# The delta rule's triangular inverse on packed 32x32 diagonal blocks instead of whole 128x128 tiles

## The chip, the core and the metric

The kernel runs on one core of a Trainium2 chip. The metric is the device time of one execution in microseconds, as the median of several runs. The engines are TensorE (PE; its weight loads are PEld), VectorE (DVE), ScalarE (ACT), GpSimd (POOL) and SyncE (SP, which issues most transfers). Each runs its own list of instructions in order, and they meet at semaphores.

## The reference

It computes one inference step of a two-layer decoder for a prompt of 512 tokens with 16 meta tokens and for 8 samples of 8 tokens. The first layer has sparse attention beside a gated DeltaNet, the second an HGRN2 recurrence; each is followed by a squared-ReLU MLP. The part that matters here is the delta rule, for every chunk and head:

```python
gam = jnp.cumsum(gg, axis=-1)
dec = jnp.exp(jnp.where(incl, gam[..., :, None] - gam[..., None, :], -jnp.inf))
kkt = jnp.einsum('bhtd,bhsd->bhts', kk, kk)
m = jnp.where(strict, bb[..., :, None] * kkt * dec, 0.0) + eye
sol = lax.linalg.triangular_solve(m, rhs, left_side=True, lower=True, unit_diagonal=True)
u, w = sol[..., :dv], sol[..., dv:]
v_new = u - jnp.einsum('bhtd,bhde->bhte', w, S)
```

## The kernel before

All 592 tokens (64 of the samples, 16 meta, 512 of the prompt) lie on the free axis of feature-major tiles. The stages follow one another: projections of layer one, convolution, attention, delta rule, output projection, MLP, the second layer, and again an MLP. The dense products stream 200 weight units of 512 KB from HBM and split each f32 operand into two fp32r halves.

The delta rule treats five token tiles, t = 0 with 80 rows (the samples and the meta tokens) and t = 1 to 4 with 128 rows, and four heads in each. It has three parts.

*Preparation* (`pe_gdn_prep`, `dve_gdn_prep`, `act_gdn_prep`): per tile the decays, the attention products (L694), the key products (L695) and transposed keys (L696). DVE makes the strictly triangular X (L716), ACT the scaled keys kd (L742) after `ebc` (L739). Each engine goes through the tiles in order.

*Inverse* (`pool_inv`, `pe_inv`, `act_inv`, `dve_inv`): the inverse of the triangular matrix I + X is built by doubling. At level l, blocks of 2^l on the diagonal are already inverted, and pairs of them are joined. T is kept as `Ti` and its transpose as `Tt`. A turn is one tile at one level: POOL masks X to the blocks that join (XL, L761), PE forms the first product (L778), ACT evicts it to P1 (L811), PE multiplies by T twice, for both orientations (L797, L799), and DVE subtracts the results from Ti and Tt (L826, L828). Level 0 has one transpose on PE instead (L785) and two subtractions from the identity (L821, L822). Four products of 128x128x128, one a head, make up each step. The list INV holds the turns, level by level and within a level tile by tile; tile 0 ends after level 3, the others after level 6. PE's order is written out: first product of turn n, then second products of turn n - 1. XL and P1 have two buffers, and PSUM banks 0 to 5 serve in pairs.

*Scan* (`pe_gdn_scan` and its partners): it starts at L852 when the whole inverse is done, and carries the state from tile to tile through Tt.

The POOL queue issues the load of the state (`sdelta`) ahead of the masks. The table of constants is loaded once at the start, on ACT's queue.

Of the kernel before, what the change touches and what calls it, by code (L numbers as in the profile page):

```python
# [21 lines left out]
ALU = mybir.AluOpType  # L22
# [3 lines left out]
P = 128  # L26
# [41 lines left out]
LEVELS = 7  # L68
HLEVELS = 7
# [3 lines left out]
def constant_table():  # L73
# [66 lines left out]
def hybrid_step(nc, x, consts, keep, at, w, wsmall, vecs, stconv, sdelta, shgrn, kvpages, ptab,  # L140
                y, krows, vrows, ikrows, convo_p, convo_s, delta_p, delta_s, hgrn_p, hgrn_s):
    ctx = ExitStack()
    with ctx:
# [582 lines left out]

        def act_gdn_prep():
            for t in range(NT):
                R, e = ROWS[t], t % 2
                nc.scalar.wait_ge(sg("gd_col"), t + 1)  # L730
                alink(nc.scalar.activation(G(G_ED)[0:R, t, :], gcol[0:R, t, 4:8], ACT.Exp))
                nc.scalar.activation(egl[:, t, :, 0:nseg(t)],
                                     ps[:, 4, 16:16 + 4 * NSEG].rearrange("p (h s) -> p h s", h=4)[:, :, 0:nseg(t)],
                                     ACT.Exp).then_inc(sg("gd_egl"), 1)
                nc.scalar.wait_ge(sg("gd_dec"), t + 1)
                nc.scalar.activation(dec[e][0:R, :, 0:R], dec[e][0:R, :, 0:R], ACT.Exp).then_inc(sg("gd_ex"), 1)
                if t:
                    nc.scalar.wait_ge(sg("gd_qk"), t)
                nc.scalar.activation(ebc[:, :, 0:R], bank(5, P, R), ACT.Exp).then_inc(sg("gd_ebc"), 1)  # L739
                nc.scalar.wait_ge(sg("gd_c"), t + 1)  # L740
                for hd in range(DNH):
                    ins = nc.scalar.activation(kd[t][0:R, hd, :], bank(0, R)[:, hd], ACT.Copy,  # L742
                                               scale=G(G_ED)[0:R, t, hd:hd + 1])
                ins.then_inc(sg("gd_kd"), 1)

        INV = [(l, t) for l in range(LEVELS) for t in range(NT) if t or l < 4]
        LAST = {t: (3 if t == 0 else LEVELS - 1) for t in range(NT)}

        def pool_inv():
            for n, (l, t) in enumerate(INV):
                R = ROWS[t]
                if l == 0:
                    nc.gpsimd.wait_ge(sg("gd_x"), t + 1)
                if n >= 2 and INV[n - 2][0] == 0:
                    nc.gpsimd.wait_ge(sg("inv_used"), n - 1)
                elif n >= 2:
                    nc.gpsimd.wait_ge(sg("inv_1"), n - 1 - NT)
                m = C(f"lev{l}")[0:R, 0:R].rearrange("p (o c) -> p o c", o=1).to_broadcast([R, 4, R])  # L760
                nc.gpsimd.tensor_tensor(XL[n % 2][0:R, :, 0:R], X[t][0:R, :, 0:R], m, ALU.mult)\  # L761
                    .then_inc(sg("inv_xl"), 1)

        def pe_inv():

            nc.tensor.wait_ge(sg("l2_rt"), 8)
            nc.tensor.wait_ge(sg("gd_kd"), NT)
            for n in range(len(INV) + 1):
                if n < len(INV):
                    l, t = INV[n]  # L770
                    R = ROWS[t]
                    nc.tensor.wait_ge(sg("inv_xl"), n + 1)
                    if l:
                        nc.tensor.wait_ge(sg("inv_used"), INV.index((l - 1, t)) + 1)
                        if n >= 2 + NT:
                            nc.tensor.wait_ge(sg("inv_p1"), n - 1 - NT)
                        for hd in range(DNH):
                            mm = nc.tensor.matmul(bank(n % 2, R, R)[:, hd], XL[n % 2][0:R, hd, 0:R],  # L778
                                                  Ti[t][0:R, hd, 0:R], start=True, stop=True)
                        mm.then_inc(sg("inv_1"), 1)  # L780
                    else:
                        if n >= 2:
                            nc.tensor.wait_ge(sg("inv_used"), n - 1)
                        for hd in range(DNH):
                            mm = nc.tensor.transpose(bank(2 + 2 * (n % 2), R, R)[:, hd], XL[n % 2][0:R, hd, 0:R],  # L785
                                                     C("ident")[0:R, 0:R])
                        mm.then_inc(sg("inv_2"), 1)
# [4 lines left out]
                R = ROWS[t]  # L792
                nc.tensor.wait_ge(sg("inv_p1"), m + 1 - NT)
                nc.tensor.wait_ge(sg("inv_used"), m - 1)
                for hd in range(DNH):
                    if l < LAST[t]:
                        nc.tensor.matmul(bank(2 + 2 * (m % 2), R, R)[:, hd], Tt[t][0:R, hd, 0:R],  # L797
                                         P1[m % 2][0:R, hd, 0:R], start=True, stop=True)
                    mm = nc.tensor.matmul(bank(3 + 2 * (m % 2), R, R)[:, hd], P1[m % 2][0:R, hd, 0:R],  # L799
                                          Tt[t][0:R, hd, 0:R], start=True, stop=True)  # L800
                mm.then_inc(sg("inv_2"), 1)

        def act_inv():
            nc.scalar.wait_ge(sg("gd_qk"), NT)
            for n, (l, t) in enumerate(INV):
                R = ROWS[t]
                if l:
                    nc.scalar.wait_ge(sg("inv_1"), n + 1 - NT)
                    if n >= 2 + NT:
                        nc.scalar.wait_ge(sg("inv_2"), n - 1)  # L810
                    nc.scalar.activation(P1[n % 2][0:R, :, 0:R], bank(n % 2, R, R), ACT.Copy)\  # L811
                        .then_inc(sg("inv_p1"), 1)

        def dve_inv(link):
            for n, (l, t) in enumerate(INV):
                R = ROWS[t]
                nc.vector.wait_ge(sg("inv_2"), n + 1)
                if l == 0:
                    i4 = C("ident")[0:R, 0:R].rearrange("p (o c) -> p o c", o=1).to_broadcast([R, 4, R])
                    nc.vector.wait_ge(sg("inv_xl"), n + 1)  # L820
                    nc.vector.tensor_tensor(Ti[t][0:R, :, 0:R], i4, bank(2 + 2 * (n % 2), R, R), ALU.subtract)  # L821
                    link(nc.vector.tensor_tensor(Tt[t][0:R, :, 0:R], i4, XL[n % 2][0:R, :, 0:R], ALU.subtract),  # L822
                         "inv_used")
                    continue
                if l < LAST[t]:
                    nc.vector.tensor_tensor(Ti[t][0:R, :, 0:R], Ti[t][0:R, :, 0:R], bank(2 + 2 * (n % 2), R, R),  # L826
                                            ALU.subtract)
                link(nc.vector.tensor_tensor(Tt[t][0:R, :, 0:R], Tt[t][0:R, :, 0:R],  # L828
                                             bank(3 + 2 * (n % 2), R, R), ALU.subtract),
                     "inv_used")  # L830

# [11 lines left out]
        def pe_gdn_scan():  # L843
            nc.tensor.wait_ge(sg("inv_used"), len(INV))
# [1335 lines left out]
```

## Time and profile before

| | us |
|---|---|
| median of 3 runs | 2011.22 |
| runs | 2010.89 to 2012.54 |
| profiled execution, its own time | 2011.88 |
| span on the core in it | 2010.1 |
| PE busy | 1811.2 (90%) |
| DVE, ACT, POOL busy | 993.0, 590.2, 281.7 |
| mean granted clock of PE | 0.925 of 2.4 GHz |

Times inside the program are counted from the span's start. A record is one instruction on the trace; an f32 product shows as two PE records with a weight load each, a transpose as one. The duration of a PE record includes its way through the pipeline, so the pace of a run of records is read from their starts.

### The profile page before, as it was taken

The numbers are of one execution on the slowest core, as the hardware profiler recorded it, in microseconds if no ns is written. First come the engines' busy times: TensorE is split into PE (matmuls) and PEld (weight loads), VectorE is DVE, ScalarE is ACT, GpSimd is POOL, SyncE is SP. The second block draws the span as 40 slices with busy tenths as digits, with TensorE's granted clock in tenths as the row PEclk, the third lists the DMA queues.
The fourth block names the chain that finished last, engine by engine and source line by source line (L and its number), as shares of the span: only waits on it lengthen the run. The fifth ranks groups of instructions, "written<-read, shape, count | busy, mean of one in ns | idle before, by whom it ended". The sixth has DMA issues, their size and how long they took to land. (4 is left out here: it accounts for less than half of the span.)

```text
span 2010.1 us, 30731 instructions
## 1 busy us (share of the span) xinstructions
PE 1811.2 (90%) x12490; PEld 1707.4 (85%) x12490; DVE 993.0 (49%) x1671; ACT 590.2 (29%) x900; POOL 281.7 (14%) x336
## 2 busy tenths in 40 slices
PE   3989878897798999999989999687879899999996
PEld 3989746795698999999989997576759899999996
DVE  3489966542336343443441111788963534434343
ACT  3234544221423221221232223433332322222221
POOL 0136200231020000000010000545512000000001
PEclk9999988795899999999999999777779999999998
DMA  5112301000121222222212222001112122222221
GB/s 167 62 53 74 122 17 43 1 1 0 68 74 64 80 78 83 75 82 83 77 61 82 83 75 72 32 32 43 43 44 72 63 85 80 77 83 82 75 83 48
DMA packets 35877, 131.75 MB, mean 66 GB/s; under 512 B 4177, under 2 KB 6433, under 8 KB 35281
## 3 DMA queue, kind: packets, MB, share of 16 engines
q1 hardware_dynamic: 34272, 121.78, 18.3%
q0 software_dynamic: 1088, 6.25, 0.9%
q10 hardware_dynamic: 432, 2.56, 0.5%
q8 instruction: 57, 0.93, 0.2%
q14 instruction: 28, 0.22, 0.0%
HBM read 119.73 MB, written 10.84 MB: 65 GB/s over the span
## 5 line engine op out<-in xcount | busy, mean ns | idle before, releaser
L363 PE MATMUL ps<-x_hi,wsp 128*128 128x296 f32 x4096 | 746.1, 303 | 30.4 <-DVE x_lo L331 27.9
L363 PEld LDWEIGHTS ps<-x_hi,wsp 128*128 128x128 f32 x4096 | 621.4, 191 | 40.7 <-issue 21.7
L345 ACT ACTIVATE wsp<-ring 128x1024 fp32r<-128x1024 f32 x200 | 211.9, 1061 | 907.3 <-PE ps L363 878.2
L363 PE MATMUL ps<-x_lo,wsp 128*128 128x296 f32 x2048 | 449.1, 301 | 0.0
L363 PE MATMUL ps<-hid,wsp 128*128 128x296 f32 x3072 | 421.1, 299 | 0.0
L363 PEld LDWEIGHTS ps<-hid,wsp 128*128 128x128 f32 x3072 | 420.3, 189 | 0.0
L349 DVE TENSOR_TENSOR wsp<-ring,wsp 128x1024 fp32r<-128x1024 f32 x200 | 249.2, 1247 | 217.2 <-ACT wsp L345 216.6
L363 PEld LDWEIGHTS ps<-x_lo,wsp 128*128 128x128 f32 x2048 | 338.1, 191 | 0.0
L417 DVE TENSOR_TENSOR h<-h,ps 128x592 f32<-128x592 f32 x80 | 61.8, 772 | 327.9 <-PE ps L363 327.9
L462 DVE TENSOR_SCALAR sq<-ps 128x592 f32<-128x592 f32 x64 | 49.6, 775 | 204.4 <-PE ps L363 204.4
L279 POOL TENSOR_TENSOR rn<-sq 128x592 f32<-128x592 f32 x4 | 7.6, 1910 | 874.3 <-ACT sq L270 874.3
L1798 PE MATMUL ps<-sq 128*128 128x128 f32 (+1 forms) x496 | 91.4, 350 | 26.3 <-DVE arena L1775 16.3
L1798 PEld LDWEIGHTS ps<-sq 128*128 128x128 f32 (+1 forms) x496 | 82.0, 253 | 32.3 <-DVE arena L1775 19.0
L1603 ACT ACTIVATE xn<-xn 128x592 f32<-128x592 f32 (+2 forms) x64 | 41.2, 658 | 90.7 <-DVE sq L1691 64.8
L449 ACT ACTIVATE hid<-sq 128x592 fp32r<-128x592 f32 x64 | 44.9, 702 | 34.7 <-DVE sq L464 34.7
L1504 PE MATMUL ps<-wsp,x_hi 128*128 128x512 f32 (+1 forms) x160 | 50.1, 394 | 1.8 <-ACT arena L385 1.8
L282 POOL TENSOR_TENSOR rn<-rn,sq 128x592 f32<-128x592 f32 x20 | 37.8, 1891 | 92.7 <-ACT sq L270 92.7
L464 DVE TENSOR_TENSOR sq<-sq 128x592 f32<-128x592 f32 x64 | 49.6, 775 | 2.2
L1640 POOL TENSOR_TENSOR xn<-xn 128x296 f32<-128x296 f32 (+2 forms) x56 | 40.9, 730 | 67.2 <-ACT xn L1603 67.2
L472 DVE TENSOR_TENSOR hid<-sq,hid 128x592 fp32r<-128x592 f32 x64 | 49.2, 769 | 0.0
L1690 DVE TENSOR_TENSOR sq<-arena,xn 128x296 f32<-128x296 f32 (+2 forms) x56 | 39.1, 699 | 19.0 <-issue 13.7
L1770 DVE COPY_PREDICATED arena<-cst,ps 128x512 f32<-128x512 int32 x64 | 46.4, 725 | 3.6 <-PE ps L1796 2.9
(308 smaller groups left out, 1912.1 us busy)
## 6 DMA issues: line engine op xcount, KB each, us to landing
ring<-in_w SPq DMA_DIRECT2D x200, 512.0 KB, 3.3
arena<-in_shgrn SPq DMA_DIRECT2D x8, 512.0 KB, 3.7
out_hgrn_s<-arena SPq DMA_DIRECT2D x8, 512.0 KB, 2.6
arena<-in_kvpages SPq DMA_DIRECT2D x16, 192.0 KB, 2.5
h<-in_x SPq DMA_DIRECT2D x4, 592.0 KB, 18.8
out_y<-xn SPq DMA_DIRECT2D x1, 2368.0 KB, 7.1
arena<-in_sdelta POOLq DMA_DIRECT2D x1, 2048.0 KB, 8.7
out_delta_s<-arena POOLq DMA_DIRECT2D x1, 2048.0 KB, 7.2
```

Of the source, the lines that this page charges most:

```text
L345: nc.scalar.activation(wsp[:, j % 2, 0, :], ring[:, j % SLOTS, :], ACT.Copy).then_inc(w_hi, 1)
L349: nc.vector.tensor_tensor(wsp[:, j % 2, 1, :], ring[:, j % SLOTS, :], wsp[:, j % 2, 0, :].bitcast(F32), ALU.subtract).then_inc(w_lo, 1)
L363: mm = nc.tensor.matmul(ps[:, 2 * (j % 2) + e, 0:HALF], a[:, k * P:(k + 1) * P], b[:, k, e * HALF:(e + 1) * HALF], start=(k == 0 and a is ...
L417: nc.vector.tensor_tensor(pairs(h[:, k, :]), pairs(h[:, k, :]), ps[:, 2 * (j % 2):2 * (j % 2) + 2, 0:HALF], ALU.add).then_inc(bank_free, 1)
L449: nc.scalar.activation(hid[:, 0, j, :], sq[:, j % 2, :], ACT.Copy).then_inc(sg("hid_hi"), 1)
L462: nc.vector.tensor_scalar(pairs(sq[:, j % 2, :]), pr, 0.0, None, ALU.max).then_inc(bank_free, 1)
L464: nc.vector.tensor_tensor(sq[:, j % 2, :], sq[:, j % 2, :], sq[:, j % 2, :], ALU.mult)\
L472: nc.vector.tensor_tensor(hid[:, 1, j, :], sq[:, j % 2, :], hid[:, 0, j, :].bitcast(F32), ALU.subtract).then_inc(sg("hid_split"), 1)
L1504: mm = nc.tensor.matmul(ps[0:ROWS[t], v_bank(a, t), :], x[:, 2 * q + k, c], w_[:, 512 * k:512 * (k + 1)], start=(q == 0 and k == 0 and x i ...
L1603: nc.scalar.activation(ee[i % 2][:, a:T], dd[i % 2][:, a:T], ACT.Exp).then_inc(sg("hg_exp"), 1)
L1770: ins = nc.vector.copy_predicated(a_[:, 1:NT, :], m.rearrange("p (o c) -> p o c", o=1) .to_broadcast([P, 4, P]), ps[:, b, :].rearrange("p ...
L1798: mm = nc.tensor.matmul(o, x_[:, c], x_[:, c], start=True, stop=True)
```

## The change

The inverse is computed on 32x32 diagonal blocks up to level 4, and levels 5 and 6 compute only the off-diagonal blocks that are missing.

ACT copies the four diagonal blocks of X into packed form Xp, 32 columns a head (`act_inv_pack`, up to four small copies for a tile). For tiles 0 to 3 the copies stand in ACT's list of the preparation, after the next tile's `ebc` and ahead of its kd. For tile 4 they stand ahead of the inverse. POOL first clears Xp of tile 0, Ti and Tt. Levels 0 to 4 (NEAR) then work on packed tiles of 128 partitions x 4 heads x 32 columns: masks, evictions and subtractions have a quarter of the columns, and one DVE subtraction serves both orientations (TT). Every product of a head becomes four products of 32x32x32 (three in tile 0), one for each diagonal block, at its own rows and columns of PE (`block_pairs`). XL and P1 have four buffers.

After a tile's last near level DVE copies the blocks into Tt and, for two blocks, Ti. The far part then runs over tiles 1 to 4 in a pipeline of four steps: q5 and v5 for the blocks that join 32 to 64, q6 and v6 for the one that joins 64 to 128. ACT evicts the q products, DVE the v products with a change of sign. The scan waits for the copies and for the last v6. The table of constants has 192 more columns: packed identity and five packed masks.

```diff
+NEAR = 5
...
+    r, c = i[:, None] % 32, np.arange(32)[None, :]
+    parts["pident"] = r == c
+    for l in range(NEAR):
+        b = 1 << l
+        parts[f"near{l}"] = (r // (2 * b) == c // (2 * b)) & (r % (2 * b) < b) & (c % (2 * b) >= b)
...
-        Ti = [region(M + 2560 + 512 * t, 4, P) for t in range(NT)]
+        Ti = Q6 = [region(M + 2560 + 512 * t, 4, 64) for t in range(NT)]
...
-        XL = [region(M + 6144, 4, P), rn[:, 0:512].rearrange("p (h c) -> p h c", h=4)]
-        P1 = [sq[:, e, 0:512].rearrange("p (h c) -> p h c", h=4) for e in range(2)]
...
+        Xp = packed(region(M + NSCR, 640), NT)
+        XL = packed(region(M + NSCR + 640, 512), 4)
+        P1 = packed(sq[:, 0, 0:512], 4)
+        TT = both(rn[:, 0:512], 2) + both(region(M + 6144, 512), 2) + both(sq[:, 1, 0:256], 1)
+        Q5 = [region(M + 2560 + 512 * t + 256, 4, 32) for t in range(NT)]
...
+        def act_inv_pack(t):
+
+            nc.scalar.wait_ge(sg("gd_x"), t + 1)
+            if t == 0:
+                nc.scalar.wait_ge(sg("inv_zero"), 1)
+            for g in range(4):
+                r = slice(32 * g, min(32 * (g + 1), ROWS[t]))
+                if r.stop > r.start:
+                    ins = nc.scalar.activation(Xp[t][r, :, 0:r.stop - r.start], X[t][r, :, r], ACT.Copy)
+            ins.then_inc(sg("inv_xp"), 1)
...
                 nc.scalar.activation(ebc[:, :, 0:R], bank(5, P, R), ACT.Exp).then_inc(sg("gd_ebc"), 1)
+                if t:
+                    act_inv_pack(t - 1)
...
-        INV = [(l, t) for l in range(LEVELS) for t in range(NT) if t or l < 4]
-        LAST = {t: (3 if t == 0 else LEVELS - 1) for t in range(NT)}
+        INV = [(l, t) for l in range(NEAR) for t in range(NT) if t or l < 4]
+        ENDS = [INV.index((3 if t == 0 else NEAR - 1, t)) + 1 for t in range(NT)]
...
+        def filled(t):
+            return 96 if t == 0 else P
+        def block_pairs(t):
+            return [(r, hd) for hd in range(DNH) for r in DIAG[0:filled(t) // 32]]
+        def inv_bank(b):
+            return ps[:, b, 0:128].rearrange("p (h c) -> p h c", h=4)
+        def inv_both(b):
+            return ps[:, b, 0:256].rearrange("p (k h c) -> p k h c", k=2, h=4)
...
+            nc.gpsimd.memset(Xp[0], 0.0).then_inc(sg("inv_zero"), 1)
+            nc.gpsimd.memset(region(M + 2560, 5 * 512), 0.0)
+            plink(nc.gpsimd.memset(region(GD, 5 * 512), 0.0), "inv_zero")
...
+                R = filled(t)
+                m = C(f"near{l}")[0:R].rearrange("p (o c) -> p o c", o=1).to_broadcast([R, 4, 32])
+                nc.gpsimd.tensor_tensor(XL[n % 4][0:R], Xp[t][0:R], m, ALU.mult).then_inc(sg("inv_xl"), 1)
...
+            nc.tensor.wait_ge(sg("gd_ebc"), NT)
...
-                        for hd in range(DNH):
-                            mm = nc.tensor.matmul(bank(n % 2, R, R)[:, hd], XL[n % 2][0:R, hd, 0:R],
-                                                  Ti[t][0:R, hd, 0:R], start=True, stop=True)
+                        for r, hd in block_pairs(t):
+                            mm = nc.tensor.matmul(inv_bank(n % 2)[r, hd], XL[n % 4][r, hd, :], TT[t][r, 0, hd, :],
+                                                  start=True, stop=True)
...
+                for r, hd in block_pairs(t):
+                    nc.tensor.matmul(inv_both(2 + m % 2)[r, 0, hd], TT[t][r, 1, hd, :], P1[m % 4][r, hd, :],
+                                     start=True, stop=True)
+                for r, hd in block_pairs(t):
+                    mm = nc.tensor.matmul(inv_both(2 + m % 2)[r, 1, hd], P1[m % 4][r, hd, :], TT[t][r, 1, hd, :],
+                                          start=True, stop=True)
...
+            for i in range(1, NT + 3):
+                if i < NT:
+                    pe_far5_q(i)
+                if 1 <= i - 1 < NT:
+                    pe_far5_v(i - 1)
+                if 1 <= i - 2 < NT:
+                    pe_far6_q(i - 2)
+                if 1 <= i - 3 < NT:
+                    pe_far6_v(i - 3)
...
+        def far_bank(b, c):
+            return ps[:, b, 0:4 * c].rearrange("p (h c) -> p h c", h=4)
+        LOWER = ((DIAG[0], DIAG[1]), (DIAG[2], DIAG[3]))
+        H0, H1 = slice(0, 64), slice(64, P)
+        FAR = [(k, i - d) for i in range(1, NT + 3) for d, k in enumerate(("q5", "v5", "q6", "v6")) if 1 <= i - d < NT]
+        TAKEN = [(w, i - d) for i in range(1, NT + 2) for d, w in ((0, 5), (2, 6)) if 1 <= i - d < NT]
...
+        def pe_far5_q(t):
+            nc.tensor.wait_ge(sg("inv_used"), ENDS[t])
+            if t > 1:
+                nc.tensor.wait_ge(sg("far_q"), taken_no(5, t - 1))
+            for hd in range(DNH):
+                for a, b in LOWER:
+                    mm = nc.tensor.matmul(far_bank(4, 32)[b, hd], X[t][a, hd, b], TT[t][a, 0, hd, :],
+                                          start=True, stop=True)
+            mm.then_inc(sg("far_mm"), 1)
+        def pe_far5_v(t):
+            nc.tensor.wait_ge(sg("far_q"), taken_no(5, t))
+            if t > 1:
+                nc.tensor.wait_ge(sg("far_v"), taken_no(5, t - 1))
+            for hd in range(DNH):
+                for a, b in LOWER:
+                    nc.tensor.matmul(far_bank(5, 32)[a, hd], Q5[t][b, hd, :], TT[t][b, 1, hd, :],
+                                     start=True, stop=True)
+                b = DIAG[1]
+                mm = nc.tensor.matmul(far_bank(5, 32)[b, hd], TT[t][b, 1, hd, :], Q5[t][b, hd, :],
+                                      start=True, stop=True)
+            mm.then_inc(sg("far_mm"), 1)
+        def pe_far6_q(t):
+            nc.tensor.wait_ge(sg("far_v"), taken_no(5, t))
+            if t > 1:
+                nc.tensor.wait_ge(sg("far_q"), taken_no(6, t - 1))
+            for hd in range(DNH):
+                mm = nc.tensor.matmul(far_bank(6, 64)[H1, hd], X[t][H0, hd, H1], Ti[t][H0, hd, :],
+                                      start=True, stop=True)
+            mm.then_inc(sg("far_mm"), 1)
+        def pe_far6_v(t):
+            nc.tensor.wait_ge(sg("far_q"), taken_no(6, t))
+            if t > 1:
+                nc.tensor.wait_ge(sg("far_v"), taken_no(6, t - 1))
+            for hd in range(DNH):
+                mm = nc.tensor.matmul(far_bank(7, 64)[H0, hd], Q6[t][H1, hd, :], Tt[t][H1, hd, H1],
+                                      start=True, stop=True)
+            mm.then_inc(sg("far_mm"), 1)
...
+                    nc.scalar.activation(P1[n % 4][0:R], inv_bank(n % 2)[0:R], ACT.Copy).then_inc(sg("inv_p1"), 1)
+            nc.scalar.wait_ge(sg("inv_zero"), 2)
+            for i in range(1, NT + 2):
+                if i < NT:
+                    nc.scalar.wait_ge(sg("far_mm"), far_no("q5", i))
+                    for a, b in LOWER:
+                        ins = nc.scalar.activation(Q5[i][b], far_bank(4, 32)[b], ACT.Copy)
+                    ins.then_inc(sg("far_q"), 1)
+                t = i - 2
+                if 1 <= t < NT:
+                    nc.scalar.wait_ge(sg("far_mm"), far_no("q6", t))
+                    nc.scalar.activation(Q6[t][H1], far_bank(6, 64)[H1], ACT.Copy).then_inc(sg("far_q"), 1)
...
+                link(nc.vector.tensor_tensor(TT[t][0:R], TT[t][0:R], inv_both(2 + n % 2)[0:R], ALU.subtract),
                      "inv_used")
+                if n + 1 == ENDS[t]:
+                    nc.vector.wait_ge(sg("inv_zero"), 2)
+                    for g, r in enumerate(DIAG[0:R // 32]):
+                        r = slice(r.start, min(r.stop, ROWS[t]))
+                        w_ = r.stop - r.start
+                        ins = nc.vector.tensor_copy(Tt[t][r, :, r], TT[t][r, 1, :, 0:w_])
+                        if t and g < 2:
+                            ins = nc.vector.tensor_copy(Ti[t][r, :, r], TT[t][r, 0])
+                    ins.then_inc(sg("inv_asm"), 1)
+            for i in range(1, NT + 2):
+                if i < NT:
+                    nc.vector.wait_ge(sg("far_mm"), far_no("v5", i))
+                    for a, b in LOWER:
+                        nc.vector.tensor_scalar(Tt[i][a, :, b], far_bank(5, 32)[a], -1.0, None, ALU.mult)
+                    b = DIAG[1]
+                    nc.vector.tensor_scalar(Ti[i][b, :, DIAG[0]], far_bank(5, 32)[b], -1.0, None, ALU.mult)\
+                        .then_inc(sg("far_v"), 1)
+                t = i - 2
+                if 1 <= t < NT:
+                    nc.vector.wait_ge(sg("far_mm"), far_no("v6", t))
+                    nc.vector.tensor_scalar(Tt[t][H0, :, H1], far_bank(7, 64)[H0], -1.0, None, ALU.mult)\
+                        .then_inc(sg("far_v"), 1)
...
-            nc.tensor.wait_ge(sg("inv_used"), len(INV))
+            nc.tensor.wait_ge(sg("inv_asm"), NT)
+            nc.tensor.wait_ge(sg("far_v"), taken_no(6, NT - 1))
```

## Rows read from the trace of the kernel before

**Rows 1.** The page: busy us (share of the span), granted PE clock in 40 slices.

```profile
PE 1811.2 (90%) x12490; PEld 1707.4 (85%) x12490; DVE 993.0 (49%) x1671; ACT 590.2 (29%) x900; POOL 281.7 (14%) x336
...
PEclk9999988795899999999999999777779999999998
```

**Rows 2.** Stages: length, busy us (records) by engine, granted clock, DMA.

```profile
347.00:372.00 25.00, 21.52 (x154) 20.86 (x153) 18.09 (x48) 9.99 (x32) 2.64 (x2) 0.85 0.01 3
372.00:381.50 9.50, 4.23 (x20) 2.82 (x20) 7.47 (x15) 0.37 (x2) 4.02 (x4) 0.66 0.00 0
381.50:395.00 13.50, 12.48 (x78) 12.27 (x79) 3.32 (x6) 2.23 (x4) 5.06 (x5) 0.61 0.00 1
395.00:453.00 58.00, 58.00 (x533) 57.86 (x531) 27.60 (x44) 14.55 (x24) 22.57 (x21) 1.00 0.01 1
```

**Rows 3.** Groups by line, 300 to 640 us: count, busy us, mean ns, idle before.

```profile
L761 POOL TENSOR_TENSOR arena<-arena,cst 128x512 f32<-128x512 f32 (+1 forms) x16 | 17.1, 1066 | 46.8 <-DVE arena L822 20.9 <-PE ps L778 19.2 <-DVE arena L716 6.6
```

**Rows 4.** Timeline (start, length, instruction) of two neighbouring turns at level 2.

```profile
405.05 0.97 PEld L778 LDWEIGHTS ps<-arena,rn 128*128 128x128 f32 x8
...
407.73 0.97 PEld L778 LDWEIGHTS ps<-arena 128*128 128x128 f32 x8
```

**Rows 5.** Timeline of the preparation's end, the inverse's start, the scan's start.

```profile
359.42 1.14 ACT L742 ACTIVATE arena<-ps,gates 128x128 f32<-128x128 f32 x4
...
361.48 0.77 PE L694 MATMUL ps<-arena 128*128 128x128 f32 x2 [0.68 <-DVE arena L716]
...
371.23 1.14 ACT L742 ACTIVATE arena<-ps,gates 128x128 f32<-128x128 f32 x4
...
372.47 0.45 PE L785 MATMUL ps<-cst,arena 80*80 80x80 f32 x4 [2.41 <-issue]
...
374.20 0.48 DVE L821 TENSOR_TENSOR arena<-cst,ps 80x320 f32<-80x320 f32 x1
...
381.53 1.36 PE L778 MATMUL ps<-arena,rn 80*80 80x80 f32 x8 [0.26 <-POOL rn L761]
...
454.02 11.15 PE L852 MATMUL ps<-arena 128*128 128x16 f32 x64 [0.97 <-DVE arena L828]
```

**Rows 6.** Timeline of two runs of small products in the attention.

```profile
328.41 0.66 PE L1203 MATMUL ps<-arena 64*32 64x256 f32 x16
...
335.26 1.01 PEld L1312 LDWEIGHTS ps<-xn,arena 128*64 128x64 f32 x32 [0.19 <-issue]
...
336.19 0.20 PEld L1316 LDWEIGHTS ps<-sq,tokm 80*64 80x64 f32 x4
```

**Rows 7.** L1203 in steps of 20 ns: PE, PEld (records in flight), clock.

```profile
328.62:328.64 0.02, 0.02 (x8) 0.00 (x0) 1.00 0.00 0
...
328.70:328.72 0.02, 0.02 (x16) 0.00 (x0) 1.00 0.00 0
```

**Rows 8.** PE in two stretches of the attention: busy us (records), clock.

```profile
334.00:338.00 4.00, 3.64 (x81) 1.00 0.00 0
328.30:338.40 10.10, 9.74 (x164) 1.00 0.01 2
```

**Rows 9.** L852, the scan's first products: PE, PEld (records), clock.

```profile
454.00:457.00 3.00, 2.98 (x27) 2.98 (x27) 1.00 0.03 5
457.00:465.20 8.20, 8.18 (x39) 8.07 (x38) 0.50 0.00 0
```

**Rows 10.** Groups by line of operations with small shapes, on DVE and POOL.

```profile
L945 DVE COPY spb<-ps 128x128 f32<-128x128 f32 x4 | 1.1, 284 | 0.0
L929 DVE TENSOR_TENSOR arena<-arena,ps 128x256 f32<-128x256 f32 x1 | 0.4, 410 | 0.0
...
L575 POOL TENSOR_TENSOR arena<-arena 128x64 f32<-128x64 f32 x36 | 18.7, 519 | 3.0
...
L1018 POOL MEMSET arena<- 128x1024 f32 x1 | 1.0, 952 | 19.7 <-PE ps L363 19.7
```

**Rows 11.** Transfers issued before 40 us: KB each, us to landing.

```profile
cst<-in_consts ACTq DMA_DIRECT2D x1, 1886.0 KB, 11.9
```

More of the change, by code:

```diff
@@ L644, in hybrid_step, with packed, both @@
         X = [region(M + 512 * t, 4, P) for t in range(NT)]
-        Ti = [region(M + 2560 + 512 * t, 4, P) for t in range(NT)]
+        Ti = Q6 = [region(M + 2560 + 512 * t, 4, 64) for t in range(NT)]
         dec = [region(M + 5120 + 512 * e, 4, P) for e in range(2)]
-        XL = [region(M + 6144, 4, P), rn[:, 0:512].rearrange("p (h c) -> p h c", h=4)]
-        P1 = [sq[:, e, 0:512].rearrange("p (h c) -> p h c", h=4) for e in range(2)]
+        def packed(v, n):
+            return [v[:, 4 * 32 * e:4 * 32 * (e + 1)].rearrange("p (h c) -> p h c", h=4) for e in range(n)]
+        def both(v, n):
+            return [v[:, 256 * e:256 * (e + 1)].rearrange("p (k h c) -> p k h c", k=2, h=4) for e in range(n)]
+        Xp = packed(region(M + NSCR, 640), NT)
[3 more added lines that the diff above has]
+        Q5 = [region(M + 2560 + 512 * t + 256, 4, 32) for t in range(NT)]
         ebc = sq[:, 1, 0:512].rearrange("p (h c) -> p h c", h=4)
@@ L744, in act_gdn_prep @@
                 ins.then_inc(sg("gd_kd"), 1)
-        INV = [(l, t) for l in range(LEVELS) for t in range(NT) if t or l < 4]
-        LAST = {t: (3 if t == 0 else LEVELS - 1) for t in range(NT)}
+        INV = [(l, t) for l in range(NEAR) for t in range(NT) if t or l < 4]
+        ENDS = [INV.index((3 if t == 0 else NEAR - 1, t)) + 1 for t in range(NT)]
+        DIAG = [slice(32 * g, 32 * (g + 1)) for g in range(4)]
+        def filled(t):
[6 more added lines that the diff above has]
+            return ps[:, b, 0:256].rearrange("p (k h c) -> p k h c", k=2, h=4)
         def pool_inv():
+            nc.gpsimd.memset(Xp[0], 0.0).then_inc(sg("inv_zero"), 1)
+            nc.gpsimd.memset(region(M + 2560, 5 * 512), 0.0)
+            plink(nc.gpsimd.memset(region(GD, 5 * 512), 0.0), "inv_zero")
             for n, (l, t) in enumerate(INV):
-                R = ROWS[t]
                 if l == 0:
[L755 to L762, printed above, removed]
+                    nc.gpsimd.wait_ge(sg("inv_xp"), t + 1)
+                if n >= 4 and INV[n - 4][0] == 0:
+                    nc.gpsimd.wait_ge(sg("inv_used"), n - 3)
+                elif n >= 4:
+                    nc.gpsimd.wait_ge(sg("inv_1"), n - 3 - NT)
+                R = filled(t)
+                m = C(f"near{l}")[0:R].rearrange("p (o c) -> p o c", o=1).to_broadcast([R, 4, 32])
+                nc.gpsimd.tensor_tensor(XL[n % 4][0:R], Xp[t][0:R], m, ALU.mult).then_inc(sg("inv_xl"), 1)
         def pe_inv():
@@ L770, in pe_inv @@
                     l, t = INV[n]
-                    R = ROWS[t]
                     nc.tensor.wait_ge(sg("inv_xl"), n + 1)
@@ L783, in pe_inv @@
                             nc.tensor.wait_ge(sg("inv_used"), n - 1)
-                        for hd in range(DNH):
-                            mm = nc.tensor.transpose(bank(2 + 2 * (n % 2), R, R)[:, hd], XL[n % 2][0:R, hd, 0:R],
-                                                     C("ident")[0:R, 0:R])
+                        for r, hd in block_pairs(t):
+                            mm = nc.tensor.matmul(inv_both(2 + n % 2)[r, 0, hd], XL[n % 4][r, hd, :], C("ident")[r, r],
+                                                  start=True, stop=True)
                         mm.then_inc(sg("inv_2"), 1)
@@ L791, in pe_inv @@
                 l, t = INV[m]
-                R = ROWS[t]
                 nc.tensor.wait_ge(sg("inv_p1"), m + 1 - NT)
                 nc.tensor.wait_ge(sg("inv_used"), m - 1)
[L795 to L800, printed above, removed]
@@ new lines, in pe_far6_q @@
+        def pe_far6_q(t):
[12 more added lines that the diff above has]
+                mm = nc.tensor.matmul(far_bank(7, 64)[H0, hd], Q6[t][H1, hd, :], Tt[t][H1, hd, H1],
+                                      start=True, stop=True)
+            mm.then_inc(sg("far_mm"), 1)
@@ L803, in act_inv @@
         def act_inv():
+            act_inv_pack(NT - 1)
             nc.scalar.wait_ge(sg("gd_qk"), NT)
             for n, (l, t) in enumerate(INV):
-                R = ROWS[t]
+                R = filled(t)
                 if l:
                     nc.scalar.wait_ge(sg("inv_1"), n + 1 - NT)
[L809 to L812, printed above, removed]
+                    if n >= 4 + NT:
+                        nc.scalar.wait_ge(sg("inv_2"), n - 3)
+                    nc.scalar.activation(P1[n % 4][0:R], inv_bank(n % 2)[0:R], ACT.Copy).then_inc(sg("inv_p1"), 1)
```

19 lines of the change are left out of this document (9 added, 10 removed).

## The prediction

> **What bounds the kernel now.** I read the page first: TensorE (PE) is busy for 90% of the span, and its granted clock is low in two places, slices 6 to 11, where attention and the delta rule lie, and a longer one in the second layer [rows 1]. The stretch of the change comes from a table by stages: the preparation, the inverse's narrowest level, its slow start, its long steady part [rows 2]. At the narrowest level PE is busy for 4.2 of 9.5 us, then it works at a lower clock, and in the last part it is busy without a gap for 58 us, so there nothing but PE's own pace counts. DVE is busy there for 27.6 us and ACT for 14.6. A mask takes GpSimd (POOL) 1.07 us [rows 3], and the timeline shows a turn to repeat every 2.68 us, from 405.05 to 407.73: one tile at one level [rows 4]. A turn is 12 products, each two records on the trace, so 24 records at 111 ns. The whole inverse has 628 records (20 single transposes, 304 products twice) and runs from 372.47 to 454.02, 81.5 us; its first product after the transposes starts at 381.53 [rows 5]. The scan and the dense stages follow with PE as the busiest engine, so I pass every microsecond of this stretch on to the end.
>
> **The change part by part.** A tile's turn becomes 3 x 16 products of 32x32x32, 96 records in place of 24. There are 24 turns in place of 32: 5 single ones, with 76 products, at level 0, and 19 full ones, with 876 products (3 x 228 at levels 1 to 3, 192 at level 4), then 112 products for the far blocks. So all hangs on what a record of this size costs, and no row shows a 32x32x32 one. The nearest has 32 moving columns too, with 64 weight columns on 128 rows: 32 of them between 335.26 and 336.19, 29 ns each, at a granted clock of 1.00 [rows 6, 8]. From below: 16 records on 64x32 sub-arrays with 256 columns run eight at a time; the count stands at 8, goes to 16 only when the second eight are under way, and the whole takes 0.66 us from 328.41 [rows 6, 7], while the 128-wide rows take 111 ns for half the columns each, one after the other. So separate sub-arrays do work at once. The new turns spread over four diagonal sub-arrays, whereas the 29 ns were on two, each taking 58 ns a record; four such would give 14.5 ns. From above: the longest dense stretch of small products has 164 records in 10.1 us, 61.6 ns each [rows 8]. I take 29 ns, the row that it is nearest to in moving columns.
>
> Level 0 starts when the last kd is there. On ACT the new copies into packed form (four of 32 partitions for a tile) stand ahead of kd; ACT takes 1.14 us for four such forms of 128 columns [rows 5], so kd of the last tile, and with it PE's start, moves from 372.47 to 373.6: +1.1. In the earlier tiles a copy delays kd, behind which PE's next key products wait; but those started 0.92 us after kd and then waited for VectorE (DVE) at 361.48 [rows 5], so 0.2 to 0.3 us may show once: nothing in the sum, 0.3 in the range. Level 0 is then 152 records, 4.4 us, to 378.0. DVE, which ends its preparation at 374.20 [rows 5], needs about 0.66 us a tile for two operations (a 128x128 copy takes 0.28 [rows 10]) and keeps up.
>
> Levels 1 to 4: 1752 records x 29 ns = 50.8 us, to 428.8. A turn is then 2.78 us of PE, no shorter than now: what goes is eight turns and the wait for masks at the start. In such a turn ACT's 0.29 us, POOL's mask (0.52 us for 64 columns [rows 10], so about 0.6) and DVE's one subtraction (0.41 us for 128x256 [rows 10]) are hidden; if PE were four times as fast, DVE would show first, at the last level with its six assembling copies, about 1.7 us a turn.
>
> Far blocks: PE's work is small (224 records, about 9 us), but it is a chain through ACT and DVE. Followed with 0.29 us an ACT copy, 0.28 us a DVE one, 0.42 us for 256 columns, and 0.3 us from PE's last product to the eviction: four tiles, of which the next q5 waits until ACT emptied the bank, and v6 of the last tile after v5, q6 and their evictions. It ends 11.9 us after the last turn, at 440.7. Now the scan starts at 454.02. So -13.3.
>
> The rest: GpSimd's clearing (two of 2560 columns at 0.95 us for 1024 [rows 10], 5 us) runs while POOL would be idle before its masks; uncovered it would shift level 0 by as much. The table of constants grows by 192 columns, 96 KB on 1886 KB that land 11.9 us after their issue [rows 11], ahead of everything: 5% of it would be 0.6, other loads share the engines; I take +0.4. No other transfer or queue order moves. Sum: 2011.9 for the profiled execution (0.7 above the median of the runs) less 13.3, plus 0.4: 1999.0.
>
> A page speaks against the change: the Trainium skill, TensorEngine Tiling (Array Packing), Instruction Overhead, gives a matmul some 60 cycles whatever its length and warns against tiling a dimension that is small already. By it, as an estimate at the higher level, a record is 25 ns, level 0 takes 3.8 us and levels 1 to 4 take 43.8, and the time would be 1991.4 in place of the 1999.0 by the row's 29 ns; the row is a little dearer than the rule.
>
> **The rivals.** *Four sub-arrays at once*: 14.5 ns a record by [rows 6, 7]. Levels 1 to 4 take 25.4 us, plus 1.3 us because DVE sets the pace at level 4, level 0 ends at 377.6 with DVE: the scan starts at 416.2, the time is 1974.5. With DVE and POOL alone as bounds (0.75 us a turn, 1.7 at level 4) it is 1966. For it: eight ran at once. Against it: only for 16 records.
>
> *Supply of records*: PE can't be given small products faster than over the long stretch, 61.6 ns [rows 8]. The 32 quick ones might have been waiting, ready, in its queue; a turn of 96 with the next behind it would use up any store. Level 0 takes 9.4 us, levels 1 to 4 take 107.9, the far part 14: the scan starts at 505, the time is 2063. It decides from where the gain of 12.9 us is eaten by 1904 records: 35.8 ns each, slower from 38. Against it: that stretch has waits and 128-column products in it. A page would make this the rule: the Trainium skill, TensorE: Matmul & The Clock Gate, Back-to-back issue gap, has a floor of 25 ns, but 62 ns where hardware decode is off; no row here tells which holds.
>
> *Lower clock*: the scan's first products load 128 columns of weights for 16 moving ones without a pause, and yet 3 us later the granted clock is at 0.50, 1.2 GHz; 27 records take 3.0 us at 2.4 GHz, the others about 219 ns each [rows 9]. The slow start of the inverse now ran at 0.61 to 0.66 as well [rows 2]. If products of 32 columns are held like that, 29 becomes 58 ns: level 0 8.8 us, levels 1 to 4 101.6, the far part 15, and 2.9 us more for the first 27 records of the scan: 2060. If it holds for a quarter of the records, the gain is gone. Against it: 81 records of 32 to 128 columns from 334 to 338 kept 1.00 [rows 8].
>
> *In between*: 36 to 50 ns a record, or part of the stage at 1.2 GHz: 2012 to 2040.
>
> **How the numbers follow.** 29 ns: 0.40, 1993 to 2005. Four at once: 0.28. In between: 0.13, of which 0.05 within 0.2% (4 us), about what this kernel's runs can tell. Lower clock throughout 0.09, supply 0.10. Faster 0.68, same 0.05, slower 0.27. The range leaves out the last two, 0.19: 1966 to 2040.
>
> **What would show it.** Right: starts about 29 ns apart within a turn of 96 records, turns of 2.8 us, PE busy throughout levels 1 to 4 at 1.00, the far part some 12 us with ACT and DVE as releasers, the scan's first product near 441. Wrong: turns of 1.4 us that wait for DVE; starts 60 ns apart with nothing awaited; a granted clock of 0.50 in the turns; kd more than 1.1 us later, or masks that PE waits for.

## The result, and the profile after

The changed kernel takes 2035.6 us (median of 4 runs, 2031.1 to 2037.7) beside 2011.6 for the kernel before: ratio 1.0116 [1.0098, 1.0134], slower by 1.2% where 1999.0 was forecast. The page of the changed kernel (span, busy time, granted clock in 40 slices, instruction queue: packets, MB, share) answers to [rows 1]:

```profile
span 2034.0 us, 33743 instructions
...
PE 1788.4 (88%) x13990; PEld 1682.6 (83%) x13990; DVE 975.6 (48%) x1684; ACT 588.9 (29%) x923; POOL 261.7 (13%) x331
...
PEclk9999988655899999999999999778779999999998
...
q8 instruction: 123, 2.02, 0.4%
```

PE and PEld have 1500 records more each, but PE is busy for 23 us less; so the time was not lost in computing. The last row is of a transfer that the forecast did not cost: the program itself, 57 packets before and 123 now, 16.4 KB each. The stages, cut at the new borders (length, PE, PEld, DVE, ACT and POOL, then granted clock and DMA), answer to [rows 2, 9]:

```profile
372.00:381.50 9.50, 5.67 (x330) 5.09 (x327) 3.04 (x11) 1.34 (x5) 3.25 (x8) 0.50 0.02 4
381.50:395.00 13.50, 7.44 (x489) 7.08 (x479) 2.10 (x5) 1.39 (x5) 2.06 (x5) 0.50 0.02 5
395.00:431.00 36.00, 17.51 (x1113) 16.17 (x1103) 9.10 (x34) 3.55 (x13) 2.89 (x7) 0.50 0.02 4
431.00:444.00 13.00, 10.46 (x208) 9.32 (x208) 6.43 (x23) 5.19 (x13) 0.00 (x0) 0.50 0.01 3
444.00:458.00 14.00, 13.71 (x64) 13.73 (x64) 0.19 (x1) 2.72 (x2) 0.00 (x0) 0.50 0.00 0
```

The clock is 0.50 from end to end. In the near levels PE is busy for 49 to 60% of the time, and no engine for more. Why shows in a timeline of PE (start, length, group, idle before and its releaser):

```profile
377.09 0.55 PE L823 MATMUL ps<-rn,arena 32*32 32x32 f32 x25 [1.62 <-issue]
377.43 0.62 PE L840 MATMUL ps<-sq,rn 32*32 32x32 f32 x24
377.86 0.57 PE L843 MATMUL ps<-rn,sq 32*32 32x32 f32 x21
378.20 0.26 PE L823 MATMUL ps<-arena 32*32 32x32 f32 x1
378.23 0.25 PE L843 MATMUL ps<-rn,sq 32*32 32x32 f32 x3
378.27 0.58 PE L823 MATMUL ps<-arena 32*32 32x32 f32 x28
378.65 0.25 PE L840 MATMUL ps<-sq,rn 32*32 32x32 f32 x1
378.66 0.25 PE L823 MATMUL ps<-arena 32*32 32x32 f32 x3
378.71 0.52 PE L840 MATMUL ps<-sq,rn 32*32 32x32 f32 x21
381.03 0.36 PE L840 MATMUL ps<-sq,rn 32*32 32x32 f32 x9 [1.80 <-issue]
```

25 records start within 0.34 us, 13.6 ns apart; then, in the middle of a group, PE stands for 1.80 us with nothing awaited. From one stall's end to the next are 127 records and 3.94 us, 31 ns a record. Such a stall comes 14 times, about every 4 us, and the instruction queue brings about one packet in each such stretch (17 from 374 to 440 us). Two of them, in GB/s in 40 slices of 0.1 us, from 378 and from 382 us on:

```profile
GB/s 0 0 164 0 0 0 0 0 0 0 0 0 0 0 0 0 0 0 0 0 0 0 0 0 0 0 0 0 0 0 0 0 0 0 0 0 0 0 0 0
GB/s 0 0 0 164 0 0 0 0 0 0 0 0 0 0 0 0 0 0 0 0 0 0 0 0 0 0 0 0 0 0 0 0 0 0 0 0 0 0 0 0
```

A packet moves within 0.1 us, so the transfer's bandwidth isn't what is short; the stalls that follow end 2.7 and 2.8 us later (381.03 and 385.19 us). What passes in between no view shows. If a packet is 127 or 128 pairs of load and product, an instruction is 64 B (16.4 KB over 256).

The scan's first product starts at 444.3 us (454.0 before, 440.7 forecast) and the first product after the delta rule (the output norm's) at 534.9 (541.1). Behind that the lead of 6.2 us is lost: from the first MLP's first ReLU on DVE to the second layer's first product of values 604.4 us pass where it was 583.5, and from the last norm product of the second layer's heads to the last residual addition 503.7 where it was 493.2. There PE stops again with nothing awaited (timeline, then windows of PE alone: length, busy, clock, DMA):

```profile
717.28 0.65 PE L369 MATMUL ps<-x_hi,wsp 128*128 128x296 f32 x2 [4.81 <-issue]
...
828.73 0.65 PE L369 MATMUL ps<-x_hi,wsp 128*128 128x296 f32 x2 [4.65 <-issue]
```

```profile
710.00:720.00 10.00, 5.19 (x31) 0.73 0.29 100
720.00:730.00 10.00, 10.00 (x70) 0.92 0.02 2
```

The two stalls lie 111 us apart, one pass of the MLP's loop, and the clock is low for a moment behind them. From 600 to 1150 us the instruction queue brings 37 packets now, 9 before.

### The profile page after: what moved, and what is told of

It reads as the page before. It is cut to its first block and busy times, and to the rows that moved or that the text cites. A ratio compares the mean times of both kernels' runs of the same rounds, so it can differ in the third digit from the quotient of the medians.

```text
span 2034.0 us, 33743 instructions
## 1 busy us (share of the span) xinstructions
PE 1788.4 (88%) x13990; PEld 1682.6 (83%) x13990; DVE 975.6 (48%) x1684; ACT 588.9 (29%) x923; POOL 261.7 (13%) x331
## 5 line engine op out<-in xcount | busy, mean ns | idle before, releaser
L369 PEld LDWEIGHTS ps<-x_hi,wsp 128*128 128x128 f32 x4096 | 628.2, 192 | 62.6 <-issue 42.2
L1830 DVE TENSOR_TENSOR sq<-arena,xn 128x296 f32<-128x296 f32 (+2 forms) x56 | 39.5, 705 | 18.3 <-issue 13.4
```

The costliest lines, as they stand in the source:

```text
L369: mm = nc.tensor.matmul(ps[:, 2 * (j % 2) + e, 0:HALF], a[:, k * P:(k + 1) * P], b[:, k, e * HALF:(e + 1) * HALF], start=(k == 0 and a is ...
L1830: nc.vector.tensor_tensor(x_[:, :, 0, :], blocks(kkall[:, hd], l)[:, :, 0, :], e_[:, :, 0, :], ALU.mult)
```

## The experiments

Two theories were open for the loss in the MLP. A: the loop's body lies at another place relative to the 16 KB packets in which code arrives, and is fetched anew in each pass. B: something else behind the delta rule, such as clock or transfers. And for the turns: the supply of code (A), the array (C), the clock (D), a turn's chain of copies and waits (E).

**Shifts.** Each kernel gets products at PE's start, where PE idles, and nothing else; counts are f32 products (four instructions) and transposes (two). One of the new instructions takes the place of a wait, so the loops move by one less than the count.

```diff
             pe.wait_ge(const_in, 32)
+            i32 = C("ident")[0:32, 0:32]
+            for _ in range(18):
+                nc.tensor.matmul(ps[0:32, 5, 0:32], i32, i32, start=True, stop=True)
+            nc.tensor.transpose(ps[0:32, 5, 0:32], i32, i32)
             pe_norm(0)
```

The changed kernel with 18 and 1:

> The changed kernel with 18 products of 32x32 and one 32x32 transpose more on TensorE at its very start, while it waits for the first norm (25.5 us of idle time there); their results are used by nothing. The change itself adds 2998 TensorE instructions ahead of the first MLP loop (3000 load and product records more, two waits less), which is 11 x 256 + 182; instruction packets are 16 KB, 256 instructions of 64 B, so these 74 more bring the loops back to the place within a packet that they had before the change. Theory A (the turns cost what their code takes to fetch, and the end is late because the MLP loops' bodies lie otherwise in the packets and are fetched again in each pass): the stalls of 4.6 to 4.8 us at the ends of the MLP's passes go, instruction packets fall from 123 to about 70, the delta rule's stage stays as it is, and the time falls by the about 21 + 10 us lost after it: 2003 to 2011 us. Theory B (the loss behind the delta rule comes from something else, such as the clock or the weights' transfers at another phase): 2031 to 2038 us and the same stalls.

The kernel before with 45 and 1:

> The kernel before, inverse and all, with 45 products of 32x32 and one 32x32 transpose more on TensorE at its very start, in the idle time before the first norm; their results are used by nothing. These are 182 instructions, what the change adds modulo 256. Theory A (place of the loops' bodies in the 16 KB packets): the MLP loops show stalls of about 4.7 us per pass as after the change, instruction packets rise from 57 to about 110, and the time rises by 20 to 31 us: 2031 to 2043 us, with not one instruction of the inverse changed. Theory B: 2010 to 2013 us, no stalls there.

The changed kernel with 64 and 0, and with 34 and 1:

> The changed kernel with 64 products of 32x32 more at TensorE's start (256 instructions, one packet), results used by nothing. Theory A with a period of 256 instructions: as the changed kernel, 2031 to 2038 us with the same stalls at the MLP's passes. If only the total of code ahead mattered, not its place in a packet, the stalls would change. Theory B: 2031 to 2038 us as well.

> The changed kernel with 34 products of 32x32 and one transpose more at TensorE's start (138 instructions: 64 behind the place that the kernel before has in its packet), results used by nothing. Theory A: a third place; the stalls are either there in full or gone in each of the two MLP loops, 2003 to 2040 us, and the instruction packets tell which (about 70 without, about 123 with both). Theory B: 2031 to 2038 us and the same stalls as in the changed kernel.

The shift by 74 gives 1996.7 us, ratio 0.9935 [0.9918, 0.9952]; the kernel before, shifted by 182, gives 2039.7, ratio 1.0149 [1.0132, 1.0166]; the shift by 256 gives 2036.0 and by 138 gives 2000.5 (one run each). Theory A holds in all four; the first is even below its range, because its near levels ran faster too. Pages of the shift by 74 and of the kernel before shifted by 182, with two lines of the latter's waits on PE (us in total, times, longest):

```profile
span 1994.9 us, 33816 instructions
...
q8 instruction: 69, 1.13, 0.2%
```

```profile
span 2038.1 us, 30912 instructions
...
q8 instruction: 112, 1.84, 0.4%
```

```profile
PE ps L363 <- issue: 10.8, 6, 2.9
PE ps L363 <- DVE h L417: 9.4, 6, 1.8
```

The kernel before has neither of the two waits; the second stands directly ahead of a stall of the first kind (1.42 us, then 2.91 us, one record apart, at 719 us). Together they are 20.2 us, and behind each stall the granted clock is low for a moment, as above. So 182 instructions in idle time cost the old kernel 28.5 us, all in its MLPs, and 74 take 39 us off the new one (32 in its MLPs, 6.3 because its scan starts at 438.0). In the latter the window that held the stall is full (PE alone):

```profile
710.00:720.00 10.00, 10.00 (x76) 1.00 0.22 75
```

Two more shifts look for the window's edges (5 products and 1 transpose; 58 and 2):

> The changed kernel with 5 products of 32x32 and one transpose more at TensorE's start (22 instructions), results used by nothing. Counted from the built program, the first MLP loop's body is 1578 instructions and the second's 1579, and they begin at 193 and 173 (modulo 256, from the program's start, to which an unknown number of instructions of the start-up comes) in the changed kernel, at 11 and 247 in the kernel before. Theory A1: a body is fetched again in each pass where it touches eight packets and stays where it touches seven, so only where it begins more than 214 (213) behind a packet's start; that fits all runs so far if the start-up has 41 to 62 instructions. Then this shift frees the first loop alone (its body begins just behind a packet's start) and leaves the second one as it is: instruction packets about 90 to 95, the 21 us of the first MLP come back and the 11 us of the second don't: 2004 to 2010 us. Theory A2 (another window, wider than 42 instructions): both loops still fetch again, 2030 to 2038 us, or both are free, 1994 to 2002 us.

> The changed kernel with 58 products of 32x32 and two transposes more at TensorE's start (236 instructions, one of which takes the place of a wait), results used by nothing. The MLP loops then begin at 172 and 152 modulo 256 (193 and 173 in the changed kernel), the mirror image of the shift by 22. A body that began at 173 and one that began at 194 were fetched in each pass, ones at 135, 115, 214 and 246 were not. By theory A1 the first loop now stalls and the second one is free: instruction packets about 95 to 98, time 2012 to 2022 us. If the window is wider than 42 instructions, both stall and it is 2030 to 2038 us.

They take 2021.1 and 2015.1 us. All placements together (start of each body modulo 256, as counted from the program's start; us between the landmarks named above, in the trace of each):

| kernel | bodies start at | first MLP | second MLP | packets |
|---|---|---|---|---|
| before | 11, 247 | 583.5 | 493.2 | 57 |
| before, shift 182 | 192, 172 | 603.8 | 501.7 | 112 |
| after | 193, 173 | 604.4 | 503.7 | 123 |
| after, shift 74 | 10, 246 | 583.5 | 492.6 | 69 |
| after, shift 138 | 74, 54 | 583.5 | 492.5 | 69 |
| after, shift 256 | 192, 172 | 605.0 | 504.6 | 124 |
| after, shift 22 | 214, 194 | 583.5 | 513.2 | 96 |
| after, shift 236 | 172, 152 | 596.5 | 493.4 | 96 |
| far part alone (below) | 135, 115 | 583.5 | 492.3 | 57 |

Bodies that start at 172 to 194 are fetched again pass by pass (27 packets more for a loop), the others never, and each loop goes by its own place. A window of 42, by which a body of 1578 instructions stays if it touches seven packets and not if it touches eight, fits all nine rows; with the edges known only to lie in 152 to 172 and 194 to 214, and the start-up's length unknown, it isn't proven. What a loop loses isn't constant, and it goes by the place too: at 172 and 173 it is 8.5 to 13 us (8.5, 10.5, 11.4 in the second loop, 13 in the first), at 192 to 194 it is 20 to 21.5 (the first loop three times, the second once), for the same number of packets. The shift by 22 missed its range for that: it moved the second loop from 173 to 194, where 20 us were lost and 11 had been assumed.

**The turns: order.** In the kernel shifted by 74:

```diff
-            return [(r, hd) for hd in range(DNH) for r in DIAG[0:filled(t) // 32]]
+            return [(r, hd) for r in DIAG[0:filled(t) // 32] for hd in range(DNH)]
```

> The changed kernel shifted by 74 instructions (so without the stalls in the MLP), and with the near products of a turn ordered by diagonal block and then by head, where they were ordered by head and then by block: four products in a row now use the same 32x32 of the array, and the count of instructions and the arithmetic are the same. Theory A (the turns run at the rate at which their code arrives, about 4 us per packet of 16 KB, 31 ns per record): records start further apart inside a burst and the stalls behind the bursts get shorter by as much; the scan's first product stays at 435 to 443 us and the time at 1993 to 2000 us. Theory C (the rate comes from four parts of the array working at once): the turns take 29 to 58 ns per record, the scan starts 5 us or more later, at 445 to 490 us, the time rises to 2003 us or more.

2003.7 us (one run), the scan starts at 443.4. Windows of 30 us in mid-turns, first with the order by block, then the kernel shifted by 74 (PE, PEld, DVE, ACT, POOL, clock):

```profile
385.00:415.00 30.00, 30.00 (x995) 29.87 (x992) 5.25 (x14) 3.05 (x11) 4.57 (x11) 0.50 0.02 4
```

```profile
385.00:415.00 30.00, 16.32 (x1026) 15.25 (x1028) 5.48 (x14) 3.04 (x11) 4.13 (x10) 0.50 0.02 4
```

On one sub-array at a time records take 30 ns and fill PE; on four in turn they take 13.6 and PE stands idle, and yet both get about 1000 records through. The stalls went as A expected. The time is C's, 3.7 us above A's range, and the scan's start lies between the two ranges. The run doesn't decide between A and C: its near levels take 58.4 us from first to last start, as in the unshifted changed kernel, and 52.4 to 56.6 in the shifts with the old order, so what the order adds can't be told from how the runs differ; and one sub-array's 30 ns happen to equal the supply's rate. What the windows show is that four at once leave nearly half of PE's time unused.

**The turns: clock.** One wide product more in each:

```diff
                 mm.then_inc(sg("inv_2"), 1)
+                nc.tensor.matmul(ps[:, 7, 0:256], C("ones"), cst[:, 0:256], start=True, stop=True)
```

> The changed kernel with one product of 128x128 weights and 256 columns more in each turn from level 1 on (19 of them, 76 instructions, which also bring the MLP loops to the place in their packets that they had before the change), into a PSUM bank that nothing reads then. Theory A (supply of code): the granted clock rises in the stage, the turns take no less time, the scan's first product stays at 436 to 443 us; the scan's 64 first products take about 11 us in place of 13.4, so 1991 to 1998 us. Theory D (the turns are as long as they are because the granted clock is 0.50): with the clock at 1.00 the 52 to 56 us of the near levels shrink by a third or more, the scan starts at 415 to 425 us, 1970 to 1982 us.

2004.7 us, the scan starts at 442.6. In the same 30 us:

```profile
385.00:415.00 30.00, 23.66 (x1002) 16.71 (x1005) 4.96 (x14) 3.04 (x11) 4.53 (x11) 0.73 0.02 4
```

The clock is 0.73 in place of 0.50 and no more records pass, against D. A's place for the scan's start holds, its time was missed: the clock fell back to 0.50 for the scan, whose first 64 products took 13.4 us again. Whether the wide products cost time of their own isn't shown; the start lies within those of the shifts (438.0 to 443.1).

**The turns: count.** Half the products with twice the columns (this kernel leaves out a part of the arithmetic), and each product twice:

```diff
+            return [(r, hd, slice(hd, hd + 2)) for hd in (0, 2) for r in DIAG[0:filled(t) // 32]]
...
+                            mm = nc.tensor.matmul(inv_bank(n % 2)[r, w_], XL[n % 4][r, hd, :], TT[t][r, 0, w_, :],
```

```diff
-            return [(r, hd) for hd in range(DNH) for r in DIAG[0:filled(t) // 32]]
+            return [(r, hd) for hd in range(DNH) for r in DIAG[0:filled(t) // 32]] * 2
```

> The changed kernel, its MLP loops shifted back to their place before the change, and in the near levels 1 to 4 one product for two heads: the weights of the first, and 64 columns, so that 438 products (876 records) stand where 876 (1752 records) stood, with the same columns in all. The second head of each pair is multiplied with the first one's weights; that part of the arithmetic is left out. Theory A (the near levels take what their code takes to arrive, about 4 us per packet of 128 load and product pairs, 31 ns per record): 1028 records with level 0 by 31 ns are 32 us, where the shifted kernel takes 52.4 us (371.3 to 423.7); the scan's first product at 415 to 422 us for 438.0, the time 1972 to 1982 us. Theory C (the columns through the array set the turns): no less than 50 us, scan start at 435 to 443 us, 1993 to 2000 us. Theory E (the chain of a turn, with its copies and waits, sets it): the same as C.

> The changed kernel, its MLP loops at their place before the change, and each near product of levels 0 to 4 issued twice into the same place (1904 records more, the result unchanged). Theory A: 1904 x 31 ns = 59 us more, the scan's first product at 490 to 502 us for 438.0, the time 2049 to 2061 us. Theory C (four parts of the array at once, records 13 ns apart inside a burst): 25 us more, 2018 to 2026 us. Theory E (the chain of a turn): less than 15 us more.

1973.8 and 2057.3 us (one run each). The scan's first products by line (durations in ns, first and last start), half and then double:

```profile
L995 PE MATMUL ps<-arena x64: 363/374/375, 415.2 to 428.6; 128*128 128x16 f32 x64
```

```profile
L992 PE MATMUL ps<-arena x64: 363/374/374, 497.3 to 510.7; 128*128 128x16 f32 x64
```

438.0 becomes 415.2 and 497.3: 1904 records more cost 59.3 us, 31 ns each (54 us and 28 ns beside the latest start among the shifts, 443.1), and fewer records with the same columns save as A said. C (25 us) and E (less than 15) are out. With half the products the clock rose; in a window of 15 us at 1.00 a record still takes 28.6 ns:

```profile
385.00:400.00 15.00, 8.55 (x524) 7.81 (x519) 6.75 (x23) 3.05 (x11) 2.91 (x7) 1.00 0.01 3
```

**The far part alone.** Old near levels, new far blocks (`LAST` keeps Ti to level 4; Q5, Q6 in free buffers):

```diff
-        INV = [(l, t) for l in range(LEVELS) for t in range(NT) if t or l < 4]
-        LAST = {t: (3 if t == 0 else LEVELS - 1) for t in range(NT)}
+        NEAR = 5
+        INV = [(l, t) for l in range(NEAR) for t in range(NT) if t or l < 4]
+        LAST = {t: (3 if t == 0 else LEVELS) for t in range(NT)}
...
+                    mm = nc.tensor.matmul(far_bank(0, 32)[b, hd], X[t][a, hd, b], Ti[t][a, hd, a],
```

> The kernel before with its levels 0 to 4 as they were, 128 wide, and only the two widest levels in the new manner (the missing far blocks alone, from the same tiles). Its MLP loops begin at 135 and 115 modulo 256, which by theory A1 is free of stalls. The eight turns of the old levels 5 and 6 at 2.68 us (21 us) go, the far part of 11 to 13 us and the wait for the last turn take their place: the scan's first product at 443 to 446 us for 454.0, at a granted clock of 1.00, and the time 2000 to 2003 us. If the packed near levels, not the far part, make the stage's gain, it stays within 3 us of the kernel before, 2008 to 2012 us; with stalls in the MLP at this place it is 2028 to 2034 us.

2009.0 us, ratio 0.999 [0.998, 1.0]. Windows of PE alone, from the end of the old turns:

```profile
400.00:434.50 34.50, 34.50 (x321) 1.00 0.01 2
434.50:440.00 5.50, 3.91 (x151) 0.95 0.02 4
440.00:447.00 7.00, 5.82 (x78) 0.50 0.01 2
447.00:460.00 13.00, 13.00 (x61) 0.50 0.00 0
```

The far part takes 12.7 us and the scan starts 7.0 us earlier, but the clock falls to 0.50 in it, ahead of the scan, where it used to fall 3 us into it [rows 9]: of the 7.0 us 2.6 are left when the output norm begins (538.5 for 541.1); the first 64 products alone lose 2.6 of the 4.4 (13.4 us from first to last start, 10.8 before). The time missed the range expected of the far part and lies in the one named for near levels that make the gain; the scan's start shows that the far part had its share as well, and 4.4 us of it are lost again by the output norm.

## Why the prediction was wrong

The step of the prediction that failed is "No other transfer or queue order moves", and with it "I pass every microsecond of this stretch on to the end". 3000 more load and product records (and two waits less) are 192 KB more of code ahead of the MLP loops and move their bodies by 182 of 256 instructions. The transfer that moved is that of the program itself: 123 instruction packets for 57, 27 of them more for each of the two loops. It costs 21 and 11 us in the two MLPs, a term that the sum hadn't. With the bodies back in place the shifts gave 1996.7 and 2000.5, where the sum says 1999.0; without, 2035.6. That the sum comes so near with the loops in place is luck in part. In the shift by 74 level 0 starts 2.3 us earlier than forecast and its near levels are 2.8 shorter, the far part is 2.4 longer and the way from the scan's start to the output norm 2.5, so four errors cancel.

- Level 0 and the constants: 373.6 was forecast, 371.5 measured (371.3 to 373.1 in the shifts). The copies on ACT did delay the last kd, by 1.3 us as forecast: it starts 1.75 us after its `ebc` (368.51, 370.26) where it was 0.48 (370.75, 371.23). But that `ebc` came 2.2 us earlier: from 347 to 351 us the granted clock was 1.00 and PE got 38 records through, where it had been 0.50 and 20. Why the clock rose earlier is open, and no term of the sum had it. The table of constants landed in 9.7 us for 11.9.
- Levels 1 to 4: 428.8 forecast, the last product starts at 429.9 (423.7 with the shift of 74, 426.7 to 429.7 in the four others). The 29 ns a record were right on the mean by luck, and wrong in their cause: PE is not busy throughout, starts are not 29 ns apart and the clock is not 1.00. *Four sub-arrays at once* was right on the array (13.6 ns) and *Supply of records* on the bound; its price of 61.6 ns came from a stretch with waits and wider products in it, 27 to 31 ns is what the supply gives.
- *Lower clock*: it did fall to 0.50 throughout, but a turn didn't feel it; the scan did.
- Far part: 11.9 forecast, 14.4 measured (12.7 in the far part alone, where it began at 1.00), with PE busy for 10.5 of 13 us at 0.50.
- The scan: 27 products at the higher clock [rows 9] are lost, 64 take 13.4 us. From its start to the output norm's products 90.6 us pass where it was 87.1. This was priced (2.9 us) only within a rival.

The packed near levels did gain: 2009.0 with the far part alone, 1996.7 with both and the loops in place.

The best version with all of the arithmetic is the changed kernel shifted by 74 instructions, 14.4 us below the kernel before and 38.8 below the unshifted one.

What stays open: what the store of code holds and how it chooses what to drop, why a loop loses 8.5 to 13 us at one place and 20 to 21.5 at another with as many packets, what a stall waits for in its last 2 us, when the latest packet has long moved, and why the near levels take 52.4 to 58.4 us and the scan starts from 438.0 to 444.3 us in runs that differ only in the shift.

## What to carry to other kernels

Count instructions as bytes to be fetched when many small operations replace a few large ones: here each load and product pair of 32x32 costs 27 to 31 ns whatever the array could do, and a turn gets shorter only with fewer of them. After a change ahead of a long loop, compare the instruction queue's packets and look for stalls with nothing awaited at the loop's passes before the change itself is blamed; a few instructions in idle time can put a loop back in place. What a stage saves is worth less if it sends the next stage into a lower clock.

## What the runs showed of the hardware

- Code arrives in packets of 16.4 KB, in the near levels one per 3.7 to 4 us, though a packet moves within 0.1 us; that is 28.6 ns a record at a clock of 1.00 and 29.2 to 31 ns at 0.50.
- A loop of 1578 PE instructions is fetched again pass by pass or not, by its place modulo 256 instructions: 27 packets and 8.5 to 21.5 us more at 172 to 194, none at ten other places from 10 to 247.
- Products on four 32x32 sub-arrays in turn start 13.6 ns apart at 1.2 GHz, on one sub-array 30 ns apart. The Trainium skill, TensorE: Matmul & The Clock Gate, Back-to-back issue gap, knows a floor of 25 ns between starts; the 13.6 ns lie below it, so for separate sub-arrays the measurement decides.
- A stream of 32x32x32 products ran at a granted clock of 0.50 from the first to the last, though records kept coming.
